# Norms of a two-block transformer: root and reciprocal on columns of tokens, spread by TensorE, and two tiles in turn while the input arrives

## The reference

```python
def rms(x, g):
    x32 = x.astype(jnp.float32)
    y = x32 * lax.rsqrt(jnp.mean(x32 * x32, axis=-1, keepdims=True) + EPS)
    return (y * g.astype(jnp.float32)).astype(x.dtype)
...
    x = x + merged @ w_out[l]
return rms_norm(x, g_final)
...
for l in range(DEPTH_2):
    ada = c_act @ w_ada[l] + b_ada[l]
    sh1, sc1, gt1, sh2, sc2, gt2 = [a[:, None, :] for a in jnp.split(ada, 6, axis=-1)]
    h = rms(x, g_mix[l]) * (1.0 + sc1) + sh1
    parts = jnp.split(h @ w_in[l], IN_SPLITS, axis=-1)
...
    x = x + gt1 * (mixed @ w_out[l])
    h2 = rms(x, g_mlp[l]) * (1.0 + sc2) + sh2
    x = x + gt2 * (jnp.square(jax.nn.relu(h2 @ w_ff1[l])) @ w_ff2[l])
```

## Time and profile before

| | us |
|---|---|
| median of 3 runs | 2622.79 (2621.53 to 2623.52) |
| the profiled execution, own time | 2620.31 |
| its span in the profile | 2618.3 |
| TensorE busy | 2389.0 (91%) |
| VectorE busy | 1454.3 (56%) |
| GpSimd busy | 1123.2 (43%) |
| ScalarE busy | 588.6 (22%) |
| share of TensorE in the chain that ended last | 67% |

### The profile page before, as it was taken

One profiled execution on the slowest core, in us unless ns is written; L12 is line 12 of the kernel. 1 busy time (PEld: TensorE's weight loads), 2 busy tenths in 40 slices (PEclk: granted clock), 3 DMA queues, 4 the chain that ended last, 5 costly groups with the idle time before them and its releaser, 6 DMA issues.

```text
span 2618.3 us, 30891 instructions
## 1 busy us (share of the span) xinstructions
PE 2389.0 (91%) x12709; PEld 1893.3 (72%) x12709; DVE 1454.3 (56%) x1774; ACT 588.6 (22%) x1200; POOL 1123.2 (43%) x672
## 2 busy tenths in 40 slices
PE   5788777888999969999998999998999999899998
PEld 3677645676666649987756888886997766688887
DVE  3889434433443567555457867747655436774341
ACT  2122234313222221124301433301114430100000
POOL 3524322234233344642115666673562205566663
PEclk8998888999999989999999999998999999999999
DMA  5324480342333532221122655532322104223331
GB/s 162 97 72 110 116 300 21 121 136 70 129 129 129 170 120 95 84 93 33 33 84 78 193 193 182 172 128 93 97 83 76 33 17 136 73 97 97 97 97 49
DMA packets 274280, 280.87 MB, mean 107 GB/s; under 512 B 29580, under 2 KB 256080, under 8 KB 274012
## 3 DMA queue, kind: packets, MB, share of 16 engines
q1 hardware_dynamic: 242012, 243.97, 29.4%
q10 hardware_dynamic: 32128, 34.92, 4.5%
HBM read 257.87 MB, written 17.85 MB: 105 GB/s over the span
## 4 chain that ended last, share of the span: by engine, by line
PE 67%; DVE 6%; ACT 1%; issue 1%; ACTq 0%; DVEq 0%
PE ps L433 43%; PE ps L1851 11%; PE ps L525 6%; PE ps L757 2%; PE ps L800 2%; PE ps L776 1%; DVE ps L864 1%; DVE normed L651 1%; DVE hT_low L641 1%; PE ps L786 1%; DVE root L646 1%; DVE ada_acc L345 1%; PE ps L627 1%; PE ps L1947 1%; PE ps L358 1%
## 5 line engine op out<-in xcount | busy, mean ns | idle before, releaser
L226 POOL TENSOR_SCALAR ring_high<-ring 128x1024 fp32r<-128x1024 f32 x302 | 337.3, 1117 | 1372.0 <-DMA ring<-in_w_in_dram 440.9
L228 POOL TENSOR_TENSOR ring_low<-ring,ring_high 128x1024 fp32r<-128x1024 f32 x302 | 757.0, 2507 | 25.2
L433 PE MATMUL ps<-hT_high,ring_high 128*128 128x512 f32 x816 | 329.2, 403 | 18.8 <-DVE hT_low L641 5.8
L433 PE MATMUL ps<-hT_low,ring_high 128*128 128x512 f32 x816 | 319.3, 391 | 0.0
L433 PE MATMUL ps<-hT_high,ring_low 128*128 128x512 f32 x816 | 319.2, 391 | 0.0
L345 DVE TENSOR_REDUCE ada_acc<-ring 128x256 f32<-128x2048 f32 x48 | 188.7, 3932 | 113.8 <-ACT ring L332 113.6
L1851 PE MATMUL ps<-ring_high,hT_high 128*128 128x256 f32 x768 | 222.5, 290 | 10.4 <-DVE hT_low L641 10.4
L1851 PE MATMUL ps<-ring_high,hT_low 128*128 128x256 f32 x768 | 220.2, 287 | 0.0
L1851 PE MATMUL ps<-ring_low,hT_high 128*128 128x256 f32 x768 | 220.2, 287 | 0.0
L332 ACT ACTIVATE ring<-ring,c_act 128x256 f32<-128x256 f32 x384 | 158.5, 497 | 187.8 <-DMA ring<-in_w_ada_dram 187.8
L433 PE MATMUL ps<-hidden_high,ring_high 128*128 128x512 f32 x512 | 200.0, 391 | 0.0
(11 more groups left out here) (342 smaller groups left out, 4163.3 us busy)
## 6 DMA issues: line engine op xcount, KB each, us to landing
ring<-in_w_in_dram SPq DMA_DIRECT2D x75, 1024.0 KB, 5.3
ring<-in_w_ff_dram SPq DMA_DIRECT2D x64, 1024.0 KB, 5.5
ring<-in_w_ada_dram SPq DMA_DIRECT2D x48, 1024.0 KB, 7.4
ring<-in_w_out_dram SPq DMA_DIRECT2D x12, 1024.0 KB, 6.6
scratch_x<-xT ACTq DMA_DIRECT2D x3, 2048.0 KB, 7.5
xT<-scratch_x ACTq DMA_DIRECT2D x3, 2048.0 KB, 8.9
ring<-in_w_mem_kv_dram SPq DMA_DIRECT2D x4, 1024.0 KB, 5.2
ring<-in_w_branch_a_dram SPq DMA_DIRECT2D x8, 512.0 KB, 6.1
```

Of the source, the lines that this page charges most:

```text
L226: nc.gpsimd.tensor_scalar(hi, raw, 1.0, 1.0, ALU.mult, ALU.mult).then_inc(hi_done.sem, 1)
L228: nc.gpsimd.tensor_tensor(lo, raw, hi.bitcast(F32), ALU.subtract).then_inc(lo_done.sem, 1)
L433: ins = nc.tensor.matmul(out[0:rows, bank, cols[0]:cols[1]], lhsT, rhs, start=start, stop=stop)
```

## The change

- Each of the four norms of block two is now made by `norm_stage`. The sum of squares is turned by TensorE into one column for each block of 128 tokens: 8 products of one column, 4 with the running sum and 4 with the last square, whose addition VectorE no longer does. Root and reciprocal run on 128x4. VectorE makes four diagonal matrices of the result, and a product with ones spreads it over the partitions, twice, into two PSUM banks. VectorE scales k = 0 and 1 from the one; ScalarE copies the other to SBUF for k = 2 to 7. Two or four products of constants stand ahead of the spreading, three behind it.
- The norm after block one and layer 0's first are made as one. ScalarE squares each residual twice (once with `g_final` as its scale), VectorE keeps two running sums, and two roots are taken on columns. The residual stream itself (`xT`) is scaled after hT is done, by 8 instructions of VectorE.
- `tiles_stage`, `Stream` and `qkv_stage` take two tiles in turn while k arrives, 6 products for each k instead of 3.
- ScalarE loads its table for the root ahead of the norm. The nine transfers of the rope tables are issued before block one's output product (layer 0) and behind the norm before layer 0's MLP (layer 1).

```diff
@@ tiles_stage
+            first = 0
+            if arriving is not None:
+                first = 2
+                size = len(tiles[0])
+                per = 1 if tiles[0][0][5][1] is None else 3
+                for j in range(0, size, per):
+                    pe.wait_ge(arriving[0].sem, arriving[1] + max(j // per + 1, arriving[3]))
+                    for n in range(2):
+                        for x in range(j, j + per):
+                            ins = product(n, x)
...
-        if act is None and ada:
+        if act is None and (ada or also is not None):
             @block.scalar
             def _(e):
                 for n in range(N):
+                    if also is not None:
+                        also(e, n)
                     for s in ada.get(n, []):
                         ada_scale(K, e, s)
@@ norm_stage, TensorE
+            def turn(bank, a, b):
+                for t in range(TT):
+                    x = slice(t * P, (t + 1) * P)
+                    nc.tensor.matmul(ps[:, bank, t:t + 1], a[:, x], K.ones[:, 0:1], start=True, stop=False)
+                    ins = nc.tensor.matmul(ps[:, bank, t:t + 1], b[:, x], K.ones[:, 0:1], start=False, stop=True)
+                ins.then_inc(turned.sem, 1)
+
+            if twice is not None:
+                squared, summed = twice[0]
+                pe.wait_ge(summed.sem, summed.total)
+                pe.wait_ge(squared.sem, squared.total - 1)
+                turn(3, twice[3], twice[4])
+                pe.wait_ge(squared.sem, squared.total)
+            turn(5, sums, last)
...
+            warm(2 if twice is None else 4)
+            pe.wait_ge(diagonal.sem, d0 + 1)
+            for j in range(2):
+                nc.tensor.matmul(bank_of(j), K.ones, diag[:, 0], start=True, stop=True).then_inc(spread.sem, 1)
+            if twice is not None:
+                nc.tensor.matmul(ps[:, 4, :], K.ones, diag[:, 1], start=True, stop=True).then_inc(spread.sem, 1)
+            warm(3)
@@ norm_stage, ScalarE
+            e.wait_ge(spread.sem, w0 + 2)
+            nc.scalar.activation(wide[:, 0, :], bank_of(1), ACT.Copy).then_inc(copied.sem, 1)
+            for k in range(KD):
+                round_up(k)
@@ norm_stage, VectorE
+            diagonals(0, nar[:, 4, :]).then_inc(diagonal.sem, 1)
...
+            e.wait_ge(spread.sem, w0 + 1)
+            for k in range(KD):
...
+                v.scalar_tensor_tensor(tmp[:, k % 2, :], src[:, k, :], gain[:, k:k + 1],
+                                       wide[:, 0, :] if k >= 2 else bank_of(0), ALU.mult, ALU.mult).then_inc(scaled.sem, 1)
@@ block_one, output product
     def out_dve(e, n, ps):
-
+        if 2 <= n:
+            e.wait_ge(squared.sem, 2 * n)
+            for x in range(2):
+                a = square[:, 0, x, :] if n == 2 else sums[x]
+                ins = v.tensor_tensor(sums[x], a, square[:, (n - 1) % 2, x, :], ALU.add)
+            ins.then_inc(summed.sem, 1)
...
+    def out_squares(e, n):
+
+        e.wait_ge(added.sem, added0 + n + 1)
+        if n >= 2:
+            e.wait_ge(summed.sem, n - 1)
+        nc.scalar.activation(square[:, n % 2, 0, :], xq[:, n, :], ACT.Square).then_inc(squared.sem, 1)
+        nc.scalar.activation(square[:, n % 2, 1, :], xq[:, n, :], ACT.Square, scale=K.g_final[:, n:n + 1]
+                             ).then_inc(squared.sem, 1)
@@ layer
-    arriving = rms_stage(K, K.xT, SEQ, gains[:, 1, :], K.hT, shift=ada[:, 24:32], summed=True)
+    arriving = norm_stage(K, K.xT, gains[:, 1, :], K.hT, ada[:, 24:32], K.sums, K.square_last)
+    if l + 1 < LAYERS:
+        rope_loads(K, T, l + 1)
```

More of the change, by code:

```diff
@@ L413, in _, with product @@
             seen = set()
+            def product(n, j):
+                bank, rows, cols, lhsT, rhs, key, start, stop = tiles[n][j]
+                out = view(n)
+                if key is not None and key not in seen:
+                    seen.add(key)
+                    K.weight_here(pe, key)
+                if rhs is None:
+                    return nc.tensor.transpose(out[0:rows, bank, cols:cols + lhsT.shape[0]], lhsT,
+                                               K.ident[0:lhsT.shape[0], 0:lhsT.shape[0]])
+                return nc.tensor.matmul(out[0:rows, bank, cols[0]:cols[1]], lhsT, rhs, start=start, stop=stop)
+            first = 0
[8 more added lines that the diff above has]
+                            ins = product(n, x)
+                        if j + per == size:
+                            ins.then_inc(made.sem, 1)
             for n, t in enumerate(tiles):
+                if n < first:
+                    continue
                 if n >= bufs:
@@ L419, in _ @@
                     pe.wait_ge(taken.sem, t0 + after[n] + 1)
[L420 to L433, removed]
+                for j in range(len(t)):
+                    ins = product(n, j)
                 ins.then_inc(made.sem, 1)
@@ L1844, in _ @@
                 K.weight_here(pe, (first + i, 2))
-                for t, tile in enumerate(token_tiles(K, first + i, K.hT)):
+                tiles = token_tiles(K, first + i, K.hT)
+                order = [(t, j) for t in range(TT) for j in range(3 * KD)]
+                if i == 0:
+                    order = [(t + u, 3 * k + x) for u in range(2) for k in range(KD) for t in (0, 2) for x in range(3)]
+                for t, j in order:
                     out = K.ps[:, (i % 4) * 2 + t // 2, (t % 2) * SLAB_W:(t % 2 + 1) * SLAB_W]
-                    for j, (_, _, _, lhsT, rhs, _, start, stop) in enumerate(tile):
-                        if i == 0 and t == 0 and j % 3 == 0:
-                            pe.wait_ge(arriving[0].sem, arriving[1] + j // 3 + 1)
-                        ins = nc.tensor.matmul(out, lhsT, rhs, start=start, stop=stop)
+                    _, _, _, lhsT, rhs, _, start, stop = tiles[t][j]
+                    if i == 0 and t == 0 and j % 3 == 0:
+                        pe.wait_ge(arriving[0].sem, arriving[1] + j // 3 + 1)
+                    ins = nc.tensor.matmul(out, lhsT, rhs, start=start, stop=stop)
                 ins.then_inc(MA.sem, 1)
@@ L1999, in _, with layer @@
                 e.dma_start(gn[:, i, :], a.broadcast_to([P, HD])).then_inc(rl.sem, 16)
-    ga.total += 1
-    K.close(vector=ga)
-    arriving = rms_stage(K, K.xT, SEQ, gains[:, 0, :], K.hT, shift=ada[:, 0:8], summed=l > 0)
+def layer(K, T, l):
+    nc, R = K.nc, K.region
+    v = nc.vector
+    gains = K.gains
+    ada = K.ada[:, l, :]
+    ga = K.sig("gains_ready")
+    rope, gn = K.rope
+    with K.stage() as block:
+        @block.vector
+        def _(e):
+            for i, (at, g) in enumerate(((8, K.g_mix[l]), (32, K.g_mlp[l]))):
+                v.scalar_tensor_tensor(gains[:, i, :], ada[:, at:at + 8], 1.0, g, ALU.add, ALU.mult)
+            if l == 0:
+                K.link(e, "gains_ready", v.tensor_scalar(gains[:, 2, :], ada[:, 16:24], 0.5, None, ALU.mult))
+                v.tensor_tensor(gains[:, 3, :], gains[:, 0, :], K.g_final, ALU.mult).then_inc(ga.sem, 1)
+            else:
+                v.tensor_scalar(gains[:, 2, :], ada[:, 16:24], 0.5, None, ALU.mult).then_inc(ga.sem, 1)
+    ga.total += 1
+    if l == 0:
+        K.close(vector=ga)
+        xq, squared, sums, last = K.outer
+        arriving = norm_stage(K, xq, gains[:, 3, :], K.hT, ada[:, 0:8], sums[1], last[1],
+                              (squared, K.g_final, K.xT, sums[0], last[0]))
+    else:
+        K.close(gains=ga)
+        arriving = norm_stage(K, K.xT, gains[:, 0, :], K.hT, ada[:, 0:8], K.sums, K.square_last)
     sx, xs = K.scratch_x.rearrange("(t p) n -> p t n", p=P), K.sig("x_spilled")
```

195 lines of the change are left out of this document (145 added, 50 removed).

## The result

| | us |
|---|---|
| before, median of 4 runs | 2623.15 (2621.53 to 2626.76) |
| changed, median of 4 runs | 2605.68 (2604.67 to 2609.51) |
| ratio, 95% interval | 0.9936 (0.9921 to 0.9952) |
| span of the profiled execution | 2602.6 |

A forecast was written before the change was run, and what follows sets the result against it. The prediction took a chain of waits, mostly TensorE's successive products broken only around the norms, as the bound; its savings summed to 34.4 us, from 2620.3 to 2585.9, plus 2.5 for the median: 2588 us, range 2573 to 2606.

The forecast's parts named there:

- First norm, 4.8: After block one's first norm: two tiles in turn leave 21 fewer products ahead of TensorE's transposes, saving 4.8 us.
- Between the blocks, 7.3 and 5.0: Layer 0's first qkv product at 973.0 instead of 980.26, 7.3 us saved; its arrival saves 5.0 more.
- the 57.9: Block one's output product: chain of residuals, squares, scalings, sums and additions, 57.9 us from 902.12 to the last square.
- the two levels of the prediction (2.7 and 5.4): Between the blocks: four products of constants, 2.7 us at the higher clock, 5.4 at the lower.
- The gap before each MLP, 3.4: Last residual to first product before each MLP of block two: 3.4 us saved, chosen between 5.0 and 0.4.
- the two bounds of the prediction (9.3 and 13.9): New gap of a single norm: 9.3 us at TensorE's higher clock, 13.9 at the lower throughout, against 14.3 before.
- Layer 0's MLP takes its gain away, -3.2: Start of layer 0's MLP: nine transfer issues delay the first relu by 3.2 us; early products buy nothing.
- Layer 1's qkv, 4.4 and 4.5: Layer 1's qkv: 4.4 us saved in the gap before it, 4.5 in its arrival through two tiles and full clock.
- its MLP's arrival, 4.8: Layer 1's MLP while k arrives: two tiles in turn leave 21 fewer products after the last low part, 4.8 us saved.
- The rival with the lower clock throughout: TensorE stays at the lower clock through every norm: 19.6 us saved, 2603 us; chance 0.13.
- The rival in which every addition waits out a GpSimd subtraction: Block one's output product: each of 12 additions takes 2.71 us instead of 0.85; 12 us saved, 2610; chance 0.05.
- The prediction's other citation of the Trainium skill: ScalarE's table loads: a drain of about 1.38 us each would save the two MLP norms 2.8 us more together.

The follow-up runs named there:

- the slabs first: In block one's output product ScalarE scales each slab ahead of the tile's squares, against the changed kernel with ring and regions in step: 2582.89 us, ratio 0.9848.
- the run with the early slabs: Layer 0's MLP's first two slabs scaled and summed earlier, against the aligned kernel with slabs ahead of squares and transfers mid-MLP (2578.35): 2579.87 us.

## Why the prediction was wrong in its size

The step that failed is one that the prediction doesn't have. The rates of the products in steady flow were taken over from the earlier trace rows as if the change couldn't touch them, and the new tile of columns and the fourth column of `gains` were put at nothing, without a word on them. The 160 bytes by which they move the ring made the products of `hidden`, `mixed` and `merged` take 0.234 us and not 0.227, which is 12.1 us in stretches where the change does nothing else. The second step, a smaller one, is the time between the blocks, which the sum had too short. With ring and regions in step the changed kernel stands at 2596, 27 us faster than before, and of the forecast 34.4 some 5 (by stretches, 29.0) to 7 (by medians) are then still missing. Term by term:

- **First norm, 4.8:** 5.1. Right; that any of it is lost on the way to the output product isn't shown (0.7 us in the mean, where each kernel differs from itself by over 3).
- **Between the blocks, 7.3 and 5.0:** 3.6 and 4.3. The chain was the one described. From the first residual (898.04) to the end of the last square (959.42) it took 61.4 us (in both profiles) and not 57.9, because three of the six pairs of additions took 3.5 to 3.8 us (the others 1.3), and I had counted 1.7 for each. (The terms written down for the 57.9 add up to 57.6.) And behind it stand 14.7 us to the first product (15.4 in the second profile), not 12.5: TensorE was at half clock for all of the turning, which took 6.96 us, where the sum had 3.8 at the higher level and 7.2 at the lower:

```profile
965.77 4.33 PE L738 MATMUL ps<-const 128*128 128x384 f32 x8
969.93 1.88 PE L743 MATMUL ps<-diagonals,const 128*128 128x512 f32 x4
```

  The eight records of the four constants took 4.33 us, between the two levels of the prediction (2.7 and 5.4), and only the spreading (1.88 for two) went at the higher one. From the first residual to the first product the forecast comes to 70.9 us, measured are 76.1 and 76.8. The kernel before took 78.1 in the profile that the forecast started from and 83.1 in its second, so how much of the 7.3 is left depends on the profile that one compares with.
- **The gap before each MLP, 3.4:** 2.8 and 2.1. From the end of the turning to the end of the diagonals it took 1.4 us, where the sum had 1.6. The spread of these gaps goes with the clock, as in the two bounds of the prediction (9.3 and 13.9): ahead of the MLPs, 9.4 us where the mean granted clock over the gap was 1.00, 10.7 with 0.84 and 12.4 with 0.72. The chosen 3.4 lay between them by judgement.
- **Layer 0's MLP takes its gain away, -3.2:** -4.4. Right in mechanism: the relu came 4.9 us (5.2 in the second profile) after the last low part, not 4.3, and TensorE stood before the column sums. One run showed the issues' share (4.9) and another that two tiles in turn are worth nothing there.
- **Layer 1's qkv, 4.4 and 4.5:** 5.1 and 5.3; **its MLP's arrival, 4.8:** 4.4. Right, and the qkv products had the full clock that was forecast.

The rival with the lower clock throughout gave 2603 and so lay nearest to the measured time, but not for its reason: the gaps were shorter than its 13.9, and the qkv arrivals ran at full clock. The rival in which every addition waits out a GpSimd subtraction was true in part: three of six pairs did in the changed kernel and four with the slabs first, by one subtraction for the pair and not for each addition. What the Trainium skill says of the shared port pair (SBUF — State Buffer, SBUF: two separate sides), that whichever instruction starts first holds it to its end, was weighed for these additions only. The cast of 2.47 us in the run with the early slabs agrees with it as well: it ended at 1431.26, 0.3 us after the GpSimd subtraction beside it.

The prediction's other citation of the Trainium skill (ScalarE: Activation LUTs, What ACT_TABLE_LOAD costs) has a drain of about 1.38 us at each table load. No row here shows one: between the blocks the changed kernel's load starts at 959.44, right behind a square that ends at 959.42, takes 1.28 us, and the next ACTIVATE starts at 960.73.

What stays open: why products whose operands are 32 bytes apart modulo 64 are slower, and whether 16 bytes or another distance would do the same. Only 0 and 32 were tried.

## What to carry to other kernels

A small tile that a change allocates moves all that lies behind it; compare the mean time of every large group of products, far from the edit too, before the gain is put down to the edit. Where ScalarE does work for a tile and work for a slab in one order, put first what depends on nothing; that order was worth 13 us here, three quarters of what the whole change gained. A stretch in which the clock moves is compared over several profiles of both kernels, since one kernel differed from itself by 3 us.

## What the runs showed of the hardware that I had not expected

- A product of 128x512 in the fast float32 form takes 0.234 us and not 0.227 when its stationary operand (the ring) and its moving one (`hidden`, `mixed`, `merged`) lie 32 bytes apart modulo 64; with both moved by the same amount it stays at 0.227. Over 2112 products, most of them on the path, this is 11.5 to 14.4 us (2634.97 and 2636.99 against 2623.44 and 2622.57). Products of two full float32 operands, ring and regions as far apart, stayed at 0.429 us a record.
- The qkv products of 256 columns, whose weights are the moving operand, stayed at 0.120 us in these kernels; there hT and the ring were moved together or not at all, so their distance was never tried.
- Two profiles of one and the same kernel (the changed one) differed by 3.3 us between S5 and the output product of block one, with a mean granted clock of 0.918 in the longer and 0.927 in the shorter; those of the kernel before by 3.2, with 0.920 and 0.926.
